# Packed gate products in the recurrence, and the first delta head's decay masks and exponentials made during the attention

## What is computed

```python
proj = u @ w_in                       # one projection for all mixers
o_na = _neighbourhood_attention(...)  # softmax(q k + bias) v over a 2-D window
# gated DeltaNet, per head and direction, per chunk:
g = jnp.cumsum(g, axis=-1)
decay = jnp.exp(jnp.where(incl, g[..., :, None] - g[..., None, :], -jnp.inf))
a_mat = jnp.einsum("bhnid,bhnjd->bhnij", k_beta, k) * jnp.where(strict, decay, 0.0)
qk = jnp.einsum("bhnid,bhnjd->bhnij", q, k) * decay
# RG-LRU gates, block-diagonal with eight 64 x 64 blocks per direction:
r = jax.nn.sigmoid(jnp.einsum("btnc,dncm->btdnm", xblk, w_r) + b_r)
i = jax.nn.sigmoid(jnp.einsum("btnc,dncm->btdnm", xblk, w_i) + b_i)
```

## Time and profile before

| what | value |
|---|---|
| median of 3 runs | 3160.93 us (3157.5 to 3161.33) |
| the profiled execution | 3162.46 us |
| its span, first to last instruction | 3160.7 us |
| PE, DVE, ACT, POOL busy | 95%, 42%, 35%, 36% |
| mean granted clock of PE | 0.98 of full speed |

### The profile page before, as it was taken

How to read it: one execution, slowest core, us unless ns; L and a number is a source line. 1 busy time by engine, 2 the same in 40 slices (tenths; PEclk the granted TensorE clock), 3 DMA queues, 4 the chain that set the end, 5 groups by cost and what they waited for, 6 DMA issues and landing times. The chain is left out here.

```text
span 3160.7 us, 44128 instructions
## 1 busy us (share of the span) xinstructions
PE 3016.8 (95%) x17907; PEld 2465.5 (78%) x17907; DVE 1326.2 (42%) x1933; ACT 1107.2 (35%) x1859; POOL 1143.1 (36%) x754
## 2 busy tenths in 40 slices
PE   5999999999999979699998999979999999999998
PEld 4778787888887746588787887868888888888887
DVE  4233233311369868577665244122223223332323
ACT  4131212232134447567655212232323333232322
POOL 4112121112111120232120343456666566666764
PEclk8999999999999989899999999989999999999999
DMA  3534232333544365210102544333232333323331
GB/s 96 173 128 140 75 109 88 110 117 99 165 162 155 125 226 155 111 52 22 72 2 72 199 160 153 117 117 107 88 99 94 94 97 123 100 89 98 98 120 63
DMA packets 239561, 353.14 MB, mean 112 GB/s; under 512 B 32896, under 2 KB 186240, under 8 KB 239360
## 3 DMA queue, kind: packets, MB, share of 16 engines
q1 hardware_dynamic: 239360, 350.32, 34.1%
HBM read 263.71 MB, written 96.36 MB: 114 GB/s over the span
## 5 line engine op out<-in xcount | busy, mean ns | idle before, releaser
L102 PE MATMUL pj_acc<-u_hi,pj_w_hi 128*128 128x512 f32 x1464 | 590.3, 403 | 15.6 <-POOL u_lo L531 13.7
L2389 DVE TENSOR_TENSOR x_tm<-m_ps,x_tm 128x512 f32<-128x512 f32 x384 | 265.0, 691 | 745.1 <-PE m_ps L104 745.1
L104 PE MATMUL pj_acc<-u_hi,pj_w_lo 128*128 128x512 f32 x1464 | 572.4, 391 | 0.0
L103 PE MATMUL pj_acc<-u_lo,pj_w_hi 128*128 128x512 f32 x1464 | 571.8, 391 | 0.0
L524 POOL TENSOR_TENSOR pj_w_lo<-pj_w_raw,pj_w_hi 128x1024 fp32r<-128x1024 f32 x61 | 150.2, 2463 | 840.4 <-ACT pj_w_hi L559 840.4
L102 PEld LDWEIGHTS pj_acc<-u_hi,pj_w_hi 128*128 128x128 f32 x1464 | 276.1, 189 | 81.9 <-POOL u_lo L531 14.5
L2266 POOL TENSOR_TENSOR m_w_lo<-m_w_raw,m_w_hi 128x1024 fp32r<-128x1024 f32 x96 | 237.8, 2500 | 263.0 <-ACT m_w_hi L2180 263.0
L103 PEld LDWEIGHTS pj_acc<-u_lo,pj_w_hi 128*128 128x128 f32 x1464 | 276.2, 189 | 65.6 <-issue 9.6
L104 PEld LDWEIGHTS pj_acc<-u_hi,pj_w_lo 128*128 128x128 f32 x1464 | 275.8, 188 | 58.4
L102 PE MATMUL m_ps<-m_v_hi,m_w_hi 128*128 128x512 f32 x768 | 300.0, 391 | 2.4 <-DVE m_v_lo L2357 2.4
L104 PE MATMUL m_ps<-m_v_hi,m_w_lo 128*128 128x512 f32 x768 | 299.7, 390 | 0.0
(11 more groups left out here) (272 smaller groups left out, 5218.3 us busy)
## 6 DMA issues: line engine op xcount, KB each, us to landing
m_w_raw<-in_w_mlp_dram SPq DMA_DIRECT2D x48, 1024.0 KB, 5.4
m_w_raw<-in_w_mlp_dram SPq DMA_DIRECT2D x96, 512.0 KB, 3.6
...
```

Source lines behind the costliest of these rows:

```text
L102: pe.matmul(out, w_hi, x_hi, start=first, stop=False)
L103: pe.matmul(out, w_hi, x_lo, start=False, stop=False)
L104: return pe.matmul(out, w_lo, x_hi, start=False, stop=last)
L2389: dve.tensor_tensor(xt, ps2[:, q % 4], xt, ALU.add).then_inc(added, 1)
```

## The change

Two parts that are independent of each other.

1. **Gates.** The block-diagonal `wbd` goes. `wri` holds for each half of the rows (one 64-channel block) the r and i weights of that block side by side, 64 x 128, in the order r, i for the upper half and i, r for the lower. `gates` issues two products of 64 rows by 128 columns at row positions 0 and 64, each into a bank of its own, where there were two of 128 rows. A bank then holds r in one half of its partitions and i in the other, so `tanh_gates` takes four activations of 64 partitions instead of two of 128. The memset of `wbd` and SP's wait for `zeroed` are gone, and two more small bias loads are issued.
2. **Head 0 of the delta net.** Its `gq` rows are loaded by SP during the attention (before the fifth bias table), its `yn` at units 28, 32 and 36. DVE makes its columns in unit 6, POOL all twelve masked tiles as soon as its masks are made and `gq` is there, and ACT one or two exponentials in each unit from 8 on, 48 in all, into a buffer that later holds `kd` and `bv`. The delta block then starts with the Gram products and `amat`. The attention's output buffer moves into `oz`.

```diff
@@ front
-        wbd = s.sb("wbd", [2, 2, 2, P])
+        wri = s.sb("wri", [2, 2, P])
...
-                        r = slice(64 * half, 64 * half + 64)
-                        sp.dma_start(wbd[r, i % 2, g, :, r], v[:, 2 * i + half].rearrange("d c m -> c d m")).then_inc(wbd_in[i % 2], 16)
+                        r, c = halves[half], halves[half ^ g]
+                        sp.dma_start(wri[r, i % 2, :, c], v[:, 2 * i + half].rearrange("d c m -> c d m")).then_inc(wri_in[i % 2], 16)
...
-            sp.wait_ge(zeroed, 4)
             for i in range(2):
                 load_blocks(i)
...
-            pool.memset(wbd[:], 0.0).then_inc(zeroed, 1)
...
-                act.activation(sg[:, sl], psg[:, 0], ACT.Tanh, bias=bias[:, 0, d, i:i + 1], scale=0.5).then_inc(r_tanh, 1)
-                act.activation(ti[:, sl], psg[:, 1], ACT.Tanh, bias=bias[:, 1, d, i:i + 1], scale=0.5).then_inc(i_tanh, 1)
+                for half, r in enumerate(halves):
+                    last = act.activation(sg[r, sl], psg[r, half], ACT.Tanh, bias=bias[r, 0, d, i:i + 1], scale=0.5)
+                last.then_inc(r_tanh, 1)
+                for half, r in enumerate(halves):
+                    o = halves[half ^ 1]
+                    last = act.activation(ti[r, sl], psg[o, half], ACT.Tanh, bias=bias[o, 1, d, i:i + 1], scale=0.5)
+                last.then_inc(i_tanh, 1)
...
-                for g in range(2):
-                    pe.matmul(psg[:, g], wbd[:, i % 2, g, d], xc[:, tb * TB:(tb + 1) * TB], start=True, stop=True).then_inc(gates_mm, 1)
+                for half, r in enumerate(halves):
+                    pe.matmul(psg[:, half], wri[r, i % 2, d], xc[r, tb * TB:(tb + 1) * TB], start=True, stop=True,
+                              tile_position=(64 * half, 0)).then_inc(gates_mm, 1)
@@ new helper, called in attention for head 0 and in columns for the others
+def decay_columns(dve, c, cols, col, ncol, cx, gq):
+    c.link(dve.tensor_copy(col, cols))
+    c.add(dve.tensor_scalar(ncol, col, -1.0, None, ALU.mult))
+    for d in range(2):
...
+        c.add(dve.tensor_copy(cx[:, d], col[:, d]))
+        c.add(dve.tensor_tensor(cx[:, 2 + d], glast, col[:, d], ALU.subtract))
+        c.add(dve.tensor_copy(cx[:, 4 + d], glast))
+    c.wait()
@@ attention
+    DG_AT, DCOL_AT, DY_AT, DEXP_AT = 1, 6, (28, 32, 36), 8
+    DEXP = 2 * 2 * NTB * 4
...
-        ot = s.sb("ot", [2, T])
+        ot = oz[:, 0:2]
...
+                if u == DG_AT:
+                    for d in range(2):
+                        sp.dma_start(gq[:, 0, d], decay_row(g_rows, 0, d)).then_inc(dg_in, 16)
+                if u in DY_AT:
+                    n = (1, 2, 0)[DY_AT.index(u)]
+                    sp.dma_start(y2[:, 0, n], dn_y[0, n]).then_inc(dy_in, 16)
...
             delta_masks(pool, mask_chain, mask_work, *masks)
+            pool.wait_ge(dg_in, 32)
+            for n in range(2 * NTB):
+                tg, d = divmod(n, 2)
+                for q, mask in enumerate((strict, incl)):
+                    pool.tensor_tensor(dd0[:, 2 * n + q], gq[:, 0, d, tg * TB:(tg + 1) * TB].rearrange("p (j n) -> p j n", n=P),
+                                       mask[:, d].unsqueeze(1).to_broadcast([P, 4, P]), ALU.add).then_inc(d_masked, 1)
...
+                if u == DCOL_AT:
+                    dve.wait_ge(dg_in, 32)
...
+                    decay_columns(dve, dc, cols[:, 0], col2[:, 0], ncol2[:, 0], cx2[:, 0], gq[:, 0])
...
+                act.wait_ge(d_masked, a + 1)
+                act.activation(dd0[:, a, j], dd0[:, a, j], ACT.Exp, bias=(col2, ncol2)[q][:, 0, d, t:t + 1],
+                               scale=(-1.0, 1.0)[q]).then_inc(d_exp, 1)
...
+                if DEXP_AT <= u < U:
+                    k, span = u - DEXP_AT, U - DEXP_AT
+                    for e in range(DEXP * k // span, DEXP * (k + 1) // span):
+                        delta_decay(e)
@@ deltanet
-        kd = s.sb("kd", [2, NT, P])
-        bv = s.sb("bv", [2, NT, P])
+        dd0 = kb[:].rearrange("p (a j) n -> p a j n", j=4)
+        kd, bv = (kb[:, 2 * NT * x:2 * NT * (x + 1)].rearrange("p (d t) n -> p d t n", d=2) for x in range(2))
...
-            load_g(0)
-            load_y(0)
+            sp.sem_inc(S["g_in"], 32)
+            sp.sem_inc(S["y_in0"], 48)
             load_z(0)
...
-            column_exp(0)
-            for n in range(2):
-                for q in range(2):
-                    exponentials(0, n, q)
+            act.sem_inc(S["cexp"], 1)
+            act.sem_inc(S["dexp"], 48)
             for step in range(STEPS):
-                for n, q in EXP_MID.get(step, ()):
-                    exponentials(0, n, q)
                 prepare(0, step)
...
-            columns(0, chains[0])
+            dve.sem_inc(S["chain"], 8)
+            chains[0].n = 8
+            dve.sem_inc(S["cols_in"], 1)
```

More of the change, by code:

```diff
@@ L266, in front @@
     r96 = slice(0, C)
+    halves = (slice(0, 64), slice(64, P))
     def lru(p, o):
@@ L458, in _ @@
             for d in range(2):
-                for g, v in enumerate((b_r, b_i)):
-                    sp.dma_start(bias[:, g, d], v[d].rearrange("(i p) -> p i", p=P), allow_slow_non_contiguous=True).then_inc(param_in, 16)
+                sp.dma_start(bias[:, 0, d], b_r[d].rearrange("(i p) -> p i", p=P), allow_slow_non_contiguous=True).then_inc(param_in, 16)
+                for half in range(2):
+                    sp.dma_start(bias[halves[half ^ 1], 1, d], b_i[d].rearrange("(i h p) -> h p i", h=2, p=64)[half],
+                                 allow_slow_non_contiguous=True).then_inc(param_in, 16)
                 sp.dma_start(lm[:, d], lam[d].rearrange("(i p) -> p i", p=P), allow_slow_non_contiguous=True).then_inc(param_in, 16)
@@ L840, in decays @@
                 c.end()
-            dve.wait_ge(zeroed, 4)
+            dve.wait_ge(zeroed, 3)
             for p in range(1, NSL + 1):
@@ L956, in groups_to @@
         return sum(group(x) is not None for x in range(u + 1))
+    strict, incl, join = masks
+    y2, gq, kb, col2, ncol2, cx2 = ahead
+    dd0 = kb[:].rearrange("p (a j) n -> p a j n", j=4)
+    DG_AT, DCOL_AT, DY_AT, DEXP_AT = 1, 6, (28, 32, 36), 8
+    DEXP = 2 * 2 * NTB * 4
     with Space(nc, "na") as s:
+        dg_in, dy_in, d_cols, d_colexp, d_masked, d_exp, d_chain = (s.sem(x) for x in (
+            "dg_in", "dy_in", "d_cols", "d_colexp", "d_masked", "d_exp", "d_chain"))
         q_in, k_in, v_in = ([[s.sem(f"{x}{a}{b}") for b in range(2)] for a in range(2)] for x in ("q_in", "k_in", "v_in"))
@@ L1212, with deltanet @@
 UN_ORDER = (0, 3, 4, 5, 1, 2)
-def deltanet(nc, proj, dn_y, g_rows, cols, masks, o_t, norm_w, ident, ones, oz):
+def deltanet(nc, proj, dn_y, g_rows, cols, masks, ahead, o_t, norm_w, ident, ones, oz):
     strict, incl, join = masks
@@ L1224, in deltanet @@
         S = {x: s.sem(x) for x in names}
-        y2 = s.sb("yn", [2, 3, T])
+        y2, gq, kb, col2, ncol2, cx2 = ahead
         with nc.sbuf_tensor("dn_th", [P, T], F32) as th:
@@ L1295, in load_g @@
                 for d in range(2):
[L1296 to L1297 removed]
+                    sp.dma_start(gq[:, h % 2, d], decay_row(g_rows, h, d)).then_inc(S["g_in"], 16)
             def load_z(h):
@@ L1341, in _ @@
             for i in range(HEADS):
-                masked(i, 0)
-                masked(i, 1)
-                masked(i, 2)
+                if i == 0:
+                    pool.sem_inc(S["masked"], 12)
+                else:
+                    masked(i, 0)
+                    masked(i, 1)
+                    masked(i, 2)
                 if i:
@@ L1349, in _ @@
                     reset(tn, n)
-                masked(i, 3)
-                masked(i, 4)
+                if i:
+                    masked(i, 3)
+                    masked(i, 4)
                 for n in range(NTB, 2 * NTB):
                     reset(tn, n)
-                masked(i, 5)
+                if i:
+                    masked(i, 5)
                 for n in UN_ORDER:
@@ L1392, in prepare @@
             def prepare(i, step):
-                for n, q in EXP_END.get(step, ()):
+                for n, q in EXP_END.get(step, ()) if i else ():
                     exponentials(i, n, q)
@@ L1652, in columns @@
             def columns(i, c):
-                col, ncol, cx = col2[:, i % 2], ncol2[:, i % 2], cx2[:, i % 2]
-                c.link(dve.tensor_copy(col, cols[:, bass.ds(i, 1)].rearrange("p a k t -> p (a k) t")))
                 dve.wait_ge(S["g_in"], i * 32 + 32)
-                c.add(dve.tensor_scalar(ncol, col, -1.0, None, ALU.mult))
-                for d in range(2):
-                    g4 = gq[:, i % 2, d].rearrange("p (t n) -> p t n", n=P)
-                    glast = g4[:, :, P - 1] if d == 0 else g4[:, :, 0]
-                    c.add(dve.tensor_copy(cx[:, d], col[:, d]))
-                    c.add(dve.tensor_tensor(cx[:, 2 + d], glast, col[:, d], ALU.subtract))
-                    c.add(dve.tensor_copy(cx[:, 4 + d], glast))
-                c.wait()
```

(7 more changed lines are left out.)

42 lines of the change are left out of this document (27 added, 15 removed).

## The result

| | before | after |
|---|---|---|
| median | 3160.82 us (4 runs) | 3140.21 us (4 runs, 3139.14 to 3141.34) |
| profiled execution, its span | 3162.46, 3160.7 us | 3140.97, 3139.3 us |

The changed kernel is 20.6 us faster, a ratio of 0.9937 with an interval of 0.992 to 0.9954. The forecast was 3138.5.

What follows compares the result with a forecast made beforehand. PE bounds projection and attention, no engine the stretch before the delta solve. Gains 13.7 (gates) + 1.8 (SP's wait) + 20 (delta start) - 13 (attention) = 22.5 us, forecast 3138.5 us; 3127 to 3152 holds 8 in 10.

Steps and rivals of the forecast that it cites:

- Gates, 13.7: Gate calls in the projection: packed products cost 1.15 instead of 1.72 us, 24 x 0.57 = 13.7 us gained; bounds 9 to 20.6.
- ACT's tanh, 0: Gate calls: four tanh instead of two lie under PE and cost nothing; if late, 12 second calls x 1.4 = 17 us.
- SP's wait, 1.8: Projection's third weight tile: without SP's wait for `zeroed` it arrives early and PE's wait goes, 1.8 us gained.
- Start of the delta block, 20: Before the delta solve: `un` starts 21.7 us earlier, less 1.7 for the clock, 20 us gained; bounds 15 and 21.7.
- Attention, 13: Extra work in the attention costs 13 us: transfers 2.5, port 6.5, ACT 2, clock 2.
- Transfers 2.5: Attention: decay rows on the full queue make DVE wait 2.5 us for the fifth table; bounds 0 and 5.
- The port, 6.5: Attention units 5 to 8: POOL's masked tiles hold up DVE's columns and `pn`, 6.5 us lost; bounds 2 and 12.
- ACT, 2: Attention: 48 added exponentials lengthen each group of four 256-wide units by 0.5, 2 us in all; bounds 0 and 8.
- R1: Rival: the attention swallows its extra work, costing 4 us there; 3129.5 us, chance 0.18.
- R2: Rival: packed gate halves don't run together between full-height fp32r products, so the gate gain is gone; 3152 us, chance 0.07.
- R3: Rival: ACT becomes the attention's bound, exponentials cost 15 us instead of 2; 3151.5 us, or 3163 at upper bounds; chance 0.11.
- R4: Rival: unit 6's stall lowers the clock, which stays low in the attention; slower, 20 units give 3194 us, chance 0.04.

Runs made afterwards that it cites:

- g_double: Changed kernel with every packed pair of gate products issued twice, the second time over the first's result; 3155.3 us (one run).
- paced_late: Changed kernel with POOL's masked tiles each waiting for DVE's output copy and the decay rows loaded three units later; 3127.2 us, ratio 0.989.
- paced: Changed kernel with POOL waiting for DVE's output copy ahead of each masked tile, one tile in three units from unit 8 on; 3128.9 us, ratio 0.9893.
- d_only: Kernel before with the second part alone: head 0 of the delta net prepared in the attention, gates as before; 3148.3 us, ratio 0.9957.
- both_wait: Changed kernel (both parts) with SP's wait for POOL's small memsets put back; 3137.6 us, ratio 0.9923.
- act_double: Kernel with paced tiles, each of the 48 exponentials preceded by a second one into a tile nobody reads; 3132.1 us, ratio 0.9906.
- g_only: Kernel before with the first part alone: packed gate products, four tanh a call, no SP wait for the zeroed blocks; 3146.7 us, ratio 0.9955.
- g_wait: Kernel before with the first part alone, but SP still waits for POOL's three small memsets; 3152.3 us (one run).

## Why the prediction came out

The forecast of 3138.5 met 3140.2, and the sum of 22.5 met 21.5 in the time of the profiled executions. That it came so near is luck in part. In those executions the front gave 14.3, the start of the delta block 20.9, the attention took 11.5 and the passages between them 0.2: 23.5 in all. The last 2.0 went in the rest, which no part of the change touches and the sum left out (1856.3 to 1858.3). The terms were off by more than the total and cancelled.

- **Gates, 13.7: measured 11.2.** Slots with two calls last 0.93 us less, not 1.1, 24 calls at 0.47. The 1.07 for a packed pair was right (1.06). The step that was mis-sized is "with it the call would cost 1.15 instead of 1.72": it has an entry and no exit, and the call costs 1.26, for the product after next pays 0.11, with its weight load not covered. g_double shows that 0.40 of a call is the price of the switch. The Trainium skill (TensorEngine Tiling, Key Properties) says that a change of tiling mode drains the engine; the 0.40 us in a call, and 0 in the second pair of g_double, agree. Without it the upper bound of 20.6 would have come.
- **ACT's tanh, 0.** Right: all 24 calls take the same 1.71 us, so PE waits for no tanh. Its upper price counted 12 second calls; there are 8, in eight slots with two calls beside eight with one.
- **SP's wait, 1.8.** The wait went; the third tile's first product is 2.9 us earlier, and 2.4 to 3.2 with the wait alone changed. The rest above 1.5 to 1.95 us is an earlier start of these executions and where the clock was low. In the total the gain can't be found.
- **Start of the delta block, 20: measured 20.9.** DVE's line stood as described; six `amat` units of 1.64 and the fills to the first `un` take 13.5 us, as forecast. `amat` begins 1.0 us later than the memset and the small column product allow. It waits for the first group of Gram products, 16 passes, which start 0.21 us apart while the granted clock is 0.50, from 1263.8 to 1267.2, and 0.11 apart behind that; the last of the 16 starts at 1266.93. At 0.11 apart they would have ended before the memset did. So this is the clock's share, 0.9 us of the sum, which had taken off 1.7 for a low clock in the solve.
- **Attention, 13: measured 11.5.** Transfers 2.5: 2.3 in unit 4, but unit 5 gives 1.8 back. The step that failed here is that the wait adds to the sum: PE, at the low clock, is behind DVE in unit 5 before (5.29 us, with DVE waiting for PE), and I read the 1.8 as work that it caught up while DVE waited for the table. paced_late, without that wait, has an attention no shorter than paced. The port, 6.5: 6.7, as unit 6 has it where it ran at full clock (3.2 to 9.9 in d_only and both_wait). In the changed kernel it has 7.9, and the other 1.2 are the low clock. The mechanism was as told, but unit 7 pays nothing, since the tiles end before it, and "if every second one waits for one tile" (three waits, 3.8 us) was four whole waits and a partial one: the columns are 5.0 us longer beside the tiles than without them (5.9 against 0.87). paced shows that the tiles are the cause. The Trainium skill (SBUF, Who interferes with whom) has DVE and GpSimd lock each other out only over the port pair that they share; the scores beside POOL's tiles, which take one input from PSUM, agree at 0.55 us. ACT, 2: at most 0.1; its 7.66 of 7.89 us in four 256-wide units (6.66 in the earlier trace rows) still fit. The clock, 2: 3.8, of which 2.6 in units 8 and 9 and 1.2 in unit 6. Units 0 to 3 and 7 have the last 0.3.
- **The rivals.** R1 fell: the attention swallowed ACT's part but not the port's. R2 fell by the call's 1.71. R3 fell, by act_double too. R4 fell: the last low stretch of the attention ends at 1161.4, and from unit 10 on the units are as before.

What a stretch of low clock does to code that no experiment touches can be read at one place of the rest, between 91 and 136 us behind the first `un`. Here it is in d_only, before and both_wait (columns as above):

```profile
1385.59:1429.07 43.48, 40.41 (x692) 33.78 (x694) 28.46 (x45) 24.22 (x47) 2.11 (x2) 1.00 0.23 93
1395.47:1440.32 44.85, 41.84 (x692) 34.95 (x694) 28.49 (x45) 24.23 (x47) 2.11 (x2) 0.96 0.23 90
1373.97:1420.49 46.52, 43.40 (x692) 36.38 (x694) 28.39 (x46) 24.20 (x47) 2.10 (x2) 0.93 0.21 86
```

It takes 43.5 us in the seven profiled executions in which the clock stays up there, 44.8 to 45.0 in the four with one stretch of 3.4 us at 0.50, and 46.5 in the one with 6.8 us. Over the whole rest, which lay between 1852.9 and 1858.3 in the twelve, the total of low clock tells nothing, though: the shortest (g_double) has 55.8 us of it and the longest (after) 54.7.

What stays open is where the low stretches fall. The same attention code took 122.4 us in g_only, 125.4 before and 125.6 in g_wait; the changed one took 134.5 in d_only, 135.7 in both_wait, 136.3 in g_double and 136.9 in the changed kernel, with the low stretches in other units each time. Whether the kernel's own timing places them or chance does is not shown, as there is one trace of each kernel. A version of the gates with fewer switches was not tried.
